# Latent attention: scores two blocks ahead in three PSUM banks, values product issued ahead of the transposes

## The reference, cut to what matters

```
def chunk_causal_softmax_attention(q, k, v):
    key_chunk = jnp.arange(seq) // CHUNK
    scale = q.shape[-1] ** -0.5
    def block(qi, t):
        allowed = key_chunk[None, :] <= (t // CHUNK)[:, None]
        s = jnp.einsum('bqhd,bshd->bhqs', qi, k).astype(jnp.float32) * scale
        p = jax.nn.softmax(jnp.where(allowed, s, NEG_INF), axis=-1)
        return jnp.einsum('bhqs,bshd->bqhd', p.astype(v.dtype), v)
    return sweep_query_blocks(block, q)
```

## Time and profile before

| what | us |
|---|---|
| median of 3 runs | 3381.57 |
| lowest, highest | 3372.29, 9482.11 |
| the profiled execution | 3381.33 |
| its span, first to last instruction | 3379.6 |
| PE busy | 3208.7 (95%) |
| DVE busy | 2717.6 (80%) |
| ACT busy | 1411.2 (42%) |
| attention stage, first layer | 176.6 to 230.3 |

### The profile page before, as it was taken

The page is one execution under the profiler, slowest core; times in us unless marked ns, Lnnn a source line. Parts: engine busy times, 40 slices in busy tenths (PEclk is TensorE's granted clock), DMA queues, the critical chain, the costliest instruction groups (busy, mean ns, idle before and its releaser), DMA issues. The chain is left out here.

```text
span 3379.6 us, 58399 instructions
## 1 busy us (share of the span) xinstructions
PE 3208.7 (95%) x20362; PEld 1966.0 (58%) x20362; DVE 2717.6 (80%) x5214; ACT 1411.2 (42%) x2117; POOL 1005.3 (30%) x754
## 2 busy tenths in 40 slices
PE   7989999999999899999799899999999998999996
PEld 3645665565666566666445465655656665666663
DVE  6866458898999788888877563688989997888887
ACT  4454443343444333333444543433444443333333
POOL 2400000332404344444324000003424144444442
PEclk9999999999999999999899999999999999999998
DMA  5103222889898999999551032338898989999994
GB/s 195 48 13 106 94 94 96 293 279 365 277 340 288 402 389 386 397 397 366 192 161 35 13 131 69 107 101 301 271 379 278 329 302 403 388 386 399 390 371 181
DMA packets 395484, 846.02 MB, mean 250 GB/s; under 512 B 34368, under 2 KB 239168, under 8 KB 394560
## 3 DMA queue, kind: packets, MB, share of 16 engines
q1 hardware_dynamic: 321024, 570.38, 47.6%
q0 software_dynamic: 73728, 268.47, 22.2%
q10 hardware_dynamic: 576, 5.37, 0.4%
HBM read 733.99 MB, written 110.10 MB: 250 GB/s over the span
## 5 line engine op out<-in xcount | busy, mean ns | idle before, releaser
L98 ACT ACTIVATE wh<-wf 128x1024 f16<-128x1024 f32 x656 | 690.8, 1053 | 947.9 <-PE ps L2132 545.8
L127 PE MATMUL ps<-xh,wh 128*128 128x384 f16 (+2 forms) x3008 | 1011.7, 336 | 78.2 <-DVEq L1273 37.4
L129 PE MATMUL ps<-xh,wl 128*128 128x384 f16 (+2 forms) x3008 | 1011.1, 336 | 0.0
L128 PE MATMUL ps<-xl,wh 128*128 128x384 f16 (+2 forms) x3008 | 1010.9, 336 | 0.0
L104 DVE SCALAR_TENSOR_TENSOR wl<-wf,wh 128x1024 f16<-128x1024 f32 x656 | 801.4, 1222 | 222.0 <-ACT wh L98 203.5
L2130 PE MATMUL ps<-work,wh 128*128 128x384 f16 x2048 | 668.9, 327 | 8.0 <-DVE work L2462 6.1
L2132 PE MATMUL ps<-work,wl 128*128 128x384 f16 x2048 | 669.2, 327 | 0.0
L2131 PE MATMUL ps<-work,wh 128*128 128x384 f16 x2048 | 669.1, 327 | 0.0
L2247 POOL DMA_INDIRECT xT<-urows,small x256 | 390.4, 1525 | 904.9 <-DVE xT L2330 650.4
L2256 POOL DMA_INDIRECT work<-experts,small x256 | 451.0, 1762 | 559.7 <-DVE work L2471 533.7
L127 PEld LDWEIGHTS ps<-xh,wh 128*128 128x128 f16 x3008 | 296.3, 99 | 303.3 <-DVEq L1273 38.4
(11 more groups left out here) (414 smaller groups left out, 3746.7 us busy)
## 6 DMA issues: line engine op xcount, KB each, us to landing
wf<-experts SPq DMA_DIRECT2D x512, 512.0 KB, 6.9
wf<-proj SPq DMA_DIRECT2D x144, 512.0 KB, 3.4
gates<-work SPq DMA_DIRECT2D x96, 512.0 KB, 8.1
work<-hid SPq DMA_DIRECT2D x256, 192.0 KB, 4.8
work<-gates SPq DMA_DIRECT2D x256, 192.0 KB, 6.3
hid<-work SPq DMA_DIRECT2D x192, 192.0 KB, 5.3
hid<-small SPq DMA_DIRECT2D x64, 192.0 KB, 5.3
xsave<-xT ACTq DMA_DIRECT2D x2, 2048.0 KB, 6.5
```

Source lines behind the costliest of these rows:

```text
L98: m.nc.scalar.activation(m.wh[:, slot, :], m.wf[:, k, :], ACT.Copy, scale=WS).then_inc(m.high_done, 1)
L127: m.nc.tensor.matmul(out, wh[:, k, :], xh[:, k, 0:n], start=(k == order[0]), stop=False)
L128: m.nc.tensor.matmul(out, wh[:, k, :], xl[:, k, 0:n], start=False, stop=False)
L129: last = m.nc.tensor.matmul(out, wl[:, k, :], xh[:, k, 0:n], start=False, stop=(k == order[-1]))
```

## The change

Three things change in the mixer, all on the same 24 blocks:

- The scores get a third bank: block i uses bank 4, 5 or 1 by i % 3, and `mla_s(i)` waits for the exponential of block i-3. To free bank 1, the input product of state-space unit 5 moves to bank 0 and waits for one more read of it.
- In iteration i PE issues `mla_s(i+2)` where it issued `mla_s(i+1)`.
- In iteration i PE issues `mla_o(i-2)` ahead of `mla_t(i-1)`, where it came behind. The one `ssm_in` of the loop moves from iteration 1 to iteration 2. The group sums behind the stage get a wait for all exponentials, which have long ended.

ACT's and DVE's programs keep their order; only the bank that they read differs.

```diff
+    def in_bank(n):
+        return B[n % 2 if n < BH else 0]
+    def score_bank(i):
+        return B[(4, 5, 1)[i % 3]]
...
             if n >= 2:
-                pe.wait_ge(m.ssm_mul, n - 1)
+                pe.wait_ge(m.ssm_mul, n - 1 if n <= BH else n)
...
-                    last = MM(cols(B[n % 2], 2 * z + i), in_weights(z, st), inputs_of(st), start=True, stop=True)
+                    last = MM(cols(in_bank(n), 2 * z + i), in_weights(z, st), inputs_of(st), start=True, stop=True)
...
-            if i >= 2:
-                pe.wait_ge(m.mla_e, i - 1)
+            if i >= 3:
+                pe.wait_ge(m.mla_e, i - 2)
             n = P * (b + 1)
-            MM(B[4 + i % 2][:, 0:n], qh[:, h, b * P:n], kh[:, h, 0:n], start=True, stop=True)\
+            MM(score_bank(i)[:, 0:n], qh[:, h, b * P:n], kh[:, h, 0:n], start=True, stop=True)\
...
         for i in range(len(iters)):
-            if i and i + 1 < len(iters):
-                mla_s(i + 1)
+            if i + 2 < len(iters):
+                mla_s(i + 2)
             if i % PIECES == 0 and i and BH + i // PIECES - 1 < UNITS:
                 ssm_out(BH + i // PIECES - 1)
             if i == 1:
                 pe.wait_ge(m.ssm_y, 2)
+            if i >= 2:
+                mla_o(i - 2)
             if i >= 1:
                 mla_t(i - 1)
-            if i >= 2:
-                mla_o(i - 2)
-            if i % PIECES == 1 and BH + i // PIECES + 1 < UNITS:
+            if i % PIECES == 2 and BH + i // PIECES + 1 < UNITS:
                 ssm_in(BH + i // PIECES + 1)
...
         def squares(i, g, c, n):
+            pe.wait_ge(m.mla_e, len(iters))
```

More of the change, by code:

```diff
@@ L1106, in scalar @@
                 act.wait_ge(m.sb_o, BH)
-            AF(prob[:, i % 2, 0:n], B[4 + i % 2][:, 0:n], ACT.Exp, scale=MLA_SCALE,
+            AF(prob[:, i % 2, 0:n], score_bank(i)[:, 0:n], ACT.Exp, scale=MLA_SCALE,
                bias=nmx[:, i % 2:i % 2 + 1], accum_out=rsum[:, i % 2:i % 2 + 1]).then_inc(m.mla_e, 1)
@@ L1361, in ssm_turn @@
             dve.wait_ge(m.ssm_bu, n + 1)
-            bu = B[n % 2].rearrange("p (z t) -> p z t", z=2)
+            bu = in_bank(n).rearrange("p (z t) -> p z t", z=2)
             TT(pr[:, 0], bu, c, ALU.mult)
@@ L1421, in mla_max @@
             dve.wait_ge(m.mla_sc, i + 1)
-            step(nc.vector.reduce_max(mx[:, k:k + 1], B[4 + k][:, 0:n], AX.X))
+            step(nc.vector.reduce_max(mx[:, k:k + 1], score_bank(i)[:, 0:n], AX.X))
             if i >= 2:
```

## The result

The changed kernel takes 3396.71 us (median of 5 runs, 3391.96 to 3403.00). The kernel before took 3372.29, 3373.04, 3380.96 and 3381.57 us in the same comparison, 3377.0 in the middle; a fifth run of it (9482 us) is disturbed and left out of the ratios. The ratio is 1.0060, 95% interval 1.0041 to 1.0079: slower by 0.6%, clear of no change, far inside 2%. A second comparison on another chip gave 3395.53 against 3376.67, ratio 1.0057 (1.0044 to 1.0070). The forecast was 3393, its range 3373 to 3404.

A forecast was written before the change was run, and what follows sets the result against it. PE was taken as nearly the bound before, a ring of waits between PE and ACT after. Ring +3.4, bank 7 copy +1.2, state-space +2.0, start +0.7: +7.3 a layer, +14.5 on 3381.3, less 3: 3393 us, range 3373 to 3404.

The forecast's parts named there:

- The ring: Attention stage: transposes, exponential, copy, values, next transposes wait in turn; 8.93 us a head against 7.60, +3.4 a layer.
- the transposes to their end: PE's transposes within the ring, counted from start to end: 1.80 us a head.
- The copy of bank 7: Values products of blocks 8 and 16 also wait for this ACT copy: 0.60 us each, twice in the ring, +1.2.
- The state-space products: Two ssm_out and one ssm_in now stand ahead of values products on PE: together up to +2.0 us a layer.
- The start: Stage start: transposes of block 1 come behind the values of block 0, +0.7 us a layer.
- The end: From the transposes of block 21 to the stage's end: about 5.1 us against 5.22 before, counted as nothing.
- The clock: PE's granted clock in the stage: stays at 1.00, new waits under 0.8 us each, counted as nothing.
- the last rival: The clock falls to half for both stages, 55 us more: 3450 us, chance 0.04.
- wake-ups: Two semaphore waits per block in the ring, 0.10 and 0.05 us: 0.60 a head; up to +9 a layer if 0.15.
- the faster rival: Scores were the wait, the ring does not bind, PE and DVE bound the stage: 3375 us, chance 0.14.
- the cheap version: Only the stage's second half pays, 2.9 us a layer: 3384 to 3387 us, chance 0.16.

The follow-up runs named there:

- e1: The change with the transposes put back ahead of the values product, third bank and early scores kept: 3368.89 us against 3375.29 before, ratio 0.9984.
- e2: The kernel before with only the values product moved ahead of the transposes, scores one block ahead in two banks: 3395.47 us, ratio 1.0054.
- e3: The full change with a third probability buffer, so an exponential waits for the transposes of three blocks back: 3373.63 us, ratio 0.9992.
- e4: The full change with ACT's copy of block i-2 issued ahead of the exponential of block i: 3374.23 us, ratio 0.9996.
- e7: The change with the middle pair of heads (blocks 8 to 15) writing values into bank 0 instead of bank 7: 3388.92 us in one run.
- e6: The change with eleven useless PE products, one per iteration from 13 on, placed between scores and values product: ratio 1.0048.
- e5: The changed kernel run again unaltered, on another chip: 3395.53 us against 3376.67 before, ratio 1.0057.
- e8: The kernel before with only the third scores bank added, scores one block ahead and transposes first: 3374.94 us against 3376.67, ratio 1.0007.
- e9: e1 with a third probability buffer and the middle pair of heads in bank 0: 3367.42 us against 3375.53 before, ratio 0.9979.

## Why the prediction was right

**The ring.** Right as a mechanism: e1 and e2 tie the loss to the swap, e3 and e4 to the exponential inside it. Its size was 8.93 us a head forecast, 9.12 measured, with 2.2 us of marked waits in place of 1.9. The term that was small is the transposes to their end: they took 0.33 + 0.44 + 0.55 + 0.65 = 1.97 us in place of the 1.80 of the earlier trace rows. Scores follow them now, where values did; e3 and e4, with the same order, show the longer times as well, and e1, with values behind them, the 0.27 and 0.60 us of before. The other terms held to 0.02 us a head in all.

**The copy of bank 7**: 0.60 each forecast; from block 13 to block 17 a head takes 9.67, 0.55 above the ring, and e7 took away 1.1 for both. **The state-space products**: 2.0 us forecast; the head with the second `ssm_out` takes 10.04 (block 9 to 13), 0.92 above the ring, and the first one (block 1 to 5, with `ssm_in`) 9.71, 0.59 above, so 1.5. **The start**: 7.93 us to the transposes of block 1 in place of 7.22, the forecast +0.7. **The end**: 5.1 forecast, 5.09 in e6, where the clock does not fall. Together the stage without the clock is 61.2 (e6), +7.5 a layer against the forecast +7.3.

**The clock** was the step that failed. It was counted at nothing, for the waits would be "under 0.8 us each, shorter than those that the stage has now". They are not all: 1.71 us at the start, 1.34 at blocks 8 and 16, 0.99 and 1.20 at the end. The forecast's own terms said so for blocks 8 and 16, with 0.7 and 0.60 on top. But no single wait decides: the kernel before has one of 1.53 us in its stage and e3 the same 1.71 at its start, both at 1.00. What sets the change apart in the rows is how many there are: PE's marked idle time in the stage rose from 5.3 us in 7 waits to 14.2 in 20. The clock was at 1.2 GHz for a part of all four stages of the change (6.6 and 3.4 us in its first profile, 13.7 in each layer of e5), and of those of e2 and e7; of the kernels without the ring (before, e1, e3, e4, e8, e9) none shows it within the stage.

By the sign that the prediction set for it (a clock under 1.00 in the stage) the last rival would hold, but its price, the clock at half for the whole stage (3450), is wrong; a partial fall is what happens, at 1.3 to 4.8 us a stage, and the prediction had no case for that.

The Trainium skill, page "TensorE: Matmul & The Clock Gate", section "A second HAM failure mode: psum-queue depth-cycling", describes, for another kernel, a clock that swings between its half and full rate through frequent short idle times between groups of matmuls. By that page the clock was to be charged, and the traces agree: 0.51 and 0.52 in single windows, 1.00 in e6 with the same ring and filled waits. The cycling through banks is not enough by itself, for e1 and e9 cycle through the same three banks at 1.00. That the short waits bring the fall rests on that, on all eight stages with the unfilled ring (change, e5, e2, e7) and on the one profile of e6; what in them decides when it comes stays open, for the falls stand at different blocks from one execution to the next.

**The number.** The forecast added 14.5 us to before; measured are some 19.7 on the first chip and 18.9 on the second. The terms without the clock come to 15.0 (2 x 7.5), so the forecast is short by about what it left out, the clock, and the measured time lies in the range because that was wide enough for it.

**Two slips in the sums**, neither of which bears on the result: wake-ups of 0.15 us each would add 3.0 us a layer and make 10.3, not 9; and the faster rival's 3375 counts from 3381.3, while the forecast and the lower end of the cheap version count from 3378.4, from which it would be 3373.

**The faster rival** would have been right for the change without its swap: e1 came to 3368.9, and the five heads to 38.6 as worked out there for PE and DVE as the bounds (38.7). **The cheap version** falls, for the first half paid in full: from block 1 to block 11 24.85 us, 21.83 before.

**The sum.** The two stages of the change's first profile are 10.0 and 8.8 us longer, 18.9 together, the span only 14.1. Of the 4.8 between them, some 2.2 and 2.5 us are missing behind the two stages, in parts which the change does not touch. The traces don't say why. The profiles here differ there in any case: from the first stage's end to the second's start they take 1621.5 to 1628.1 us, and behind the second 1462.9 to 1474.7. It stays open. In the stick-breaking part ahead of the stage the clock also falls, in the kernel before too, in one layer or the other and by 2.3 us; in the two profiles these cancel.

## What to carry to other kernels

When two instructions of a pipeline are swapped on one engine, write down for each what stands between it and the one that it depends on, and follow the wait through every engine's own order until it comes back: here values, copy, exponential, transposes and values again, each in its turn. A step earlier for one input (the scores) is worth something only if no such ring is longer than the busiest engine's work. This ring could be cut at three of its links, by the order on PE (e1), the order on ACT (e4) or one buffer (e3), and the first was worth most.

## What was not expected

With waits mostly of 0.3 to 1.3 us, and none over 1.71, the granted clock went to 1.2 GHz in parts of every stage of the change. With eleven useless products in those of the second half it stayed at 2.4 GHz, and the stage was 1.3 to 4.8 us shorter, in the one profile that there is of it.

The third bank gave exactly nothing alone (53.73 and 53.74 us against 53.73), and the repeat from layer to layer is to 0.01 us wherever the clock stays: 50.39 and 50.38, 51.94 and 51.94.
